# The scan's products of states and queries: one plain fp32 matmul each, or three passes over split operands

## The reference, cut to what matters

```python
states = jnp.einsum('bclgn,bclgr,bclgrp->bcgrpn', b_c, to_end, x_c)
chunk_decay = jnp.exp(a_cum[:, :, -1]).astype(dtype)
def carry_state(state, inp):
    st, dec = inp
    return state * dec[..., None, None] + st, state
_, h_in = lax.scan(carry_state, h0, (...states..., ...chunk_decay...))
y_off = jnp.einsum('bclgn,bcgrpn,bclgr->bclgrp', c_c, h_in, jnp.exp(a_cum).astype(dtype))
return (y_diag + y_off).reshape(bsz, s, g, r, p)
```

## Time and profile before

| | |
|---|---|
| time, median of 3 runs | 2360.77 us (2360.46 to 2361.38) |
| profiled execution | 2362.43 us |
| its span in the trace | 2360.6 us |
| mean granted TensorE clock over the span | 0.997 |
| instructions | 35337 |

### The profile page before, as it was taken

The page is one execution under the profiler, slowest core; times in us unless marked ns, Lnnn a source line. Parts: engine busy times, 40 slices in busy tenths (PEclk is TensorE's granted clock), DMA queues, the critical chain, the costliest instruction groups (busy, mean ns, idle before and its releaser), DMA issues.

```text
span 2360.6 us, 35337 instructions
## 1 busy us (share of the span) xinstructions
PE 2328.3 (99%) x14096; PEld 2017.1 (85%) x14096; DVE 1640.0 (69%) x2369; ACT 1241.5 (53%) x2034; POOL 267.1 (11%) x210
## 2 busy tenths in 40 slices
PE   8999999999999999999999999999999999999998
PEld 7777778766788888899988899998887888899997
DVE  5698846478775455687786788785677555777784
ACT  7777764355663344455554555554544354455552
POOL 0000000555100000100002200001033201100002
PEclk9999999999999999999999999999999999999999
DMA  6221335323566232233233243223322232333322
GB/s 199 81 72 52 89 106 176 118 74 113 188 217 213 86 125 67 90 113 108 90 99 107 81 125 108 87 84 108 115 64 63 90 116 72 107 108 108 93 69 90
DMA packets 177269, 251.97 MB, mean 107 GB/s; under 512 B 9936, under 2 KB 101328, under 8 KB 177104
## 3 DMA queue, kind: packets, MB, share of 16 engines
q1 hardware_dynamic: 175952, 248.13, 33.6%
q10 hardware_dynamic: 1152, 1.57, 0.2%
HBM read 231.83 MB, written 16.78 MB: 105 GB/s over the span
## 4 chain that ended last, share of the span: by engine, by line
PE 94%; DVE 3%; ACT 2%; issue 1%; DMA 1%; POOL 0%; SPq 0%; DVEq 0%; POOLq 0%; ACTq 0%
PE bank L1485 92%; PE bank L1647 1%; DVE wlo L2498 1%; PE bank L1670 0%; ACT whi L1886 0%; DMA zb<-scr_z 0%; PE bank L1768 0%; PE bank L1792 0%; DVE T L2506 0%; PE bank L1611 0%; DMA raw<-in_w_in 0%; DVE xg L2502 0%; ACT E L2153 0%; POOL xw L3411 0%; ACT pr L1887 0%
## 5 line engine op out<-in xcount | busy, mean ns | idle before, releaser
L1485 PE MATMUL bank<-xopr,shi 128*128 128x256 f32 x3360 | 605.0, 283 | 0.0
L1485 PEld LDWEIGHTS bank<-xopr,shi 128*128 128x128 f32 x3360 | 524.5, 192 | 0.5
L1485 PE MATMUL bank<-xopr,slo 128*128 128x256 f32 x1680 | 475.4, 283 | 0.0
L2498 DVE TENSOR_TENSOR wlo<-raw,whi 128x1024 fp32r<-128x1024 f32 (+2 forms) x286 | 351.7, 1234 | 128.3 <-ACT whi L1886 127.6
L1485 PE MATMUL bank<-xh,whi 128*128 128x512 f32 x1016 | 407.8, 401 | 7.2 <-DVE wlo L2498 7.2
L1485 PE MATMUL bank<-xh,wlo 128*128 128x512 f32 x1016 | 397.3, 391 | 0.0
L1485 PE MATMUL bank<-xl,whi 128*128 128x512 f32 x1016 | 397.2, 391 | 0.0
L1886 ACT ACTIVATE whi<-raw 128x1024 fp32r<-128x1024 f32 (+2 forms) x286 | 292.9, 1031 | 142.6 <-PE bank L1485 125.4
L1485 PEld LDWEIGHTS bank<-xopr,slo 128*128 128x128 f32 x1680 | 322.5, 192 | 0.0
L1485 PEld LDWEIGHTS bank<-xh,whi 128*128 128x128 f32 x1016 | 191.4, 188 | 49.8 <-DVE wlo L2498 8.1
L1485 PEld LDWEIGHTS bank<-xh,wlo 128*128 128x128 f32 x1016 | 191.1, 188 | 41.6
(11 more groups left out here) (396 smaller groups left out, 4341.9 us busy)
## 6 DMA issues: line engine op xcount, KB each, us to landing
raw<-in_w_in SPq DMA_DIRECT2D x92, 512.0 KB, 3.7
quarter<-in_w_ffn_in SPq DMA_DIRECT2D x32, 512.0 KB, 4.7
quarter<-in_ffn_gate SPq DMA_DIRECT2D x32, 512.0 KB, 3.8
quarter<-in_ffn_up SPq DMA_DIRECT2D x32, 512.0 KB, 4.8
raw<-in_ffn_down SPq DMA_DIRECT2D x28, 512.0 KB, 4.5
raw<-in_w_xattn_kv SPq DMA_DIRECT2D x16, 512.0 KB, 4.1
raw<-in_w_kv_mem SPq DMA_DIRECT2D x16, 512.0 KB, 4.7
raw<-in_w_branch_ssd SPq DMA_DIRECT2D x16, 512.0 KB, 4.7
```

The source lines that it names most:

```text
L1485: return e.matmul(out, l, r, start=start, stop=stop, skip_group_check=skip)
L2498: return e.tensor_tensor(out, a, b, op)
```

## The change

Each product of a state and the queries is made from split operands in three passes. ACT copies the queries of a group to `CTh` and each state to one of two buffers `Hh` as fp32r; DVE subtracts, and writes the lower parts in place: `CTl` over `CT`, `Hl` over `HF` or `HB`. `ct_split` is a step at the fourth state of a group, `h_split` number 0 at the sixth, and number k + 1 just ahead of product k.

```diff
+        Hl = [[None] + [at_kb(142 + 2 * i, [P, S], F32R, name="Hl") for i in range(3)],
+              [at_kb(148 + 2 * i, [P, S], F32R, name="Hl") for i in range(3)] + [None]]
+        Hh = [at_kb(kb, [P, S], F32R, name="Hh") for kb in (126, 214)]
+        CTh, CTl = at_kb(216, [P, S], F32R, name="CTh"), at_kb(190, [P, 4, S], F32R, name="CTl")
...
                 step("state", g, i)
+                if i == 3:
+                    step("ct_split", g)
+                if i == 5:
+                    step("h_split", g, 0)
                 yield
+        ACROSS = [(c, d) for c in range(4) for d in range(2) if (d, c) not in ((0, 0), (1, 3))]
...
+                    if (c, d) in ACROSS:
+                        k = ACROSS.index((c, d))
+                        if k < 5:
+                            step("h_split", g, k + 1)
                         side.new("off", g, c, d, among=ELSE)
                         step("across", g, c, d)
                         yield
...   (PE)
-                w.wait_ge(*at("h in", g, d, c))
-                mm(b[:], CT[:, g, chunk(c)], (HF, HB)[d][c][:], True, True).then_inc(*up("off", ("off", g, c, d)))
+                w.wait_ge(*at("ct lo", g))
+                w.wait_ge(*at("h lo", g, c, d))
+                hi = Hh[ACROSS.index((c, d)) % 2]
+                mm(b[:], CTh[:, chunk(c)], hi[:], True, False)
+                mm(b[:], CTh[:, chunk(c)], Hl[d][c][:], False, False)
+                mm(b[:], CTl[:, g, chunk(c)], hi[:], False, True).then_inc(*up("off", ("off", g, c, d)))
...   (ACT)
+            def ct_split(g):
+                w.wait_ge(*at("cb", g))
+                if g:
+                    w.wait_ge(*at("off", g - 1, 3, 0))
+                copy(CTh[:], CT[:, g, :]).then_inc(*up("h_first", ("ct hi", g)))
+            def h_split(g, k):
+                c, d = ACROSS[k]
+                w.wait_ge(*at("h in", g, d, c))
+                if k > 1:
+                    w.wait_ge(*at("off", g, *ACROSS[k - 2]))
+                elif g:
+                    w.wait_ge(*at("off", g - 1, 3, 0))
+                copy(Hh[k % 2][:], (HF, HB)[d][c][:]).then_inc(*up("h_first", ("h hi", g, c, d)))
...   (DVE)
+            def ct_split(g):
+                w.wait_ge(*at("ct hi", g))
+                tt(CTl[:, g, :], CT[:, g, :], CTh[:].bitcast(F32), ALU.subtract).then_inc(*up("h_in", ("ct lo", g)))
+            def h_split(g, k):
+                c, d = ACROSS[k]
+                w.wait_ge(*at("h decay", g, 5))
+                w.wait_ge(*at("h hi", g, c, d))
+                tt(Hl[d][c][:], (HF, HB)[d][c][:], Hh[k % 2][:].bitcast(F32), ALU.subtract).then_inc(
+                    *up("h_in", ("h lo", g, c, d)))
```

More of the change, by code:

```diff
@@ L834, in across @@
                 for d in range(2):
-                    if (d, c) not in ((0, 0), (1, 3)):
+                    if (c, d) in ACROSS:
+                        k = ACROSS.index((c, d))
+                        if k < 5:
+                            step("h_split", g, k + 1)
                         side.new("off", g, c, d, among=ELSE)
@@ L2477, in scalar @@
                     "k_split": k_split, "q_split": q_split,
-                    "o_split": o_split, "dt": dt, "cum": cum, "difference": difference, "pick": pick, "cb": cb, "state": state_, "decay": decay, "z_out": z_out,
+                    "o_split": o_split, "dt": dt, "cum": cum, "difference": difference, "pick": pick, "ct_split": ct_split, "h_split": h_split, "cb": cb, "state": state_, "decay": decay, "z_out": z_out,
                     "z_square": z_square, "y_mean": y_mean, "y_turn": y_turn, "bs_out": bs_out, "m_split": m_split,
@@ L3388, in vector @@
                     "conv_in": conv_in, "conv": conv, "silu_mul": silu_mul, "dt_turn": dt_turn, "gate": gate,
-                    "gate_out": gate_out, "o_split": o_split, "ba_out": ba_out, "dt": dt, "cum": cum, "difference": difference, "skip": skip,
+                    "gate_out": gate_out, "o_split": o_split, "ba_out": ba_out, "dt": dt, "cum": cum, "difference": difference, "ct_split": ct_split, "h_split": h_split, "skip": skip,
                     "state": state_, "decay": decay, "decayed": decayed, "y_add": y_add, "across": across_, "z_silu": z_silu, "z_gate": z_gate,
```

## The result

| | before | changed |
|---|---|---|
| median (range), 4 runs each | 2361.07 us (2360.46 to 2362.54) | 2382.95 us (2380.52 to 2383.63) |
| span of the profiled execution | 2360.6 us | 2381.8 us |
| granted clock over the span | 0.997 | 0.994 |

The ratio is 1.0091, 95% interval 1.0079 to 1.0103: the change costs 21.9 us. The forecast was slower by 8.0, with a range up to 2379. The sign held and the size didn't.

The account below looks back on a forecast made before the run. TensorE, busy 99%, bounds the kernel, with VectorE's chain beside or ahead of it late in the scan. Unabsorbed VectorE work 10.7, less lead 2.5, less group 0's 0.15, gives +8.0 us: 2368.8 us, range 2357 to 2379.

Parts of the forecast that it names:

- The bound by stage: Scan: chain VectorE, ScalarE, VectorE lies beside TensorE in groups 1 and 2, ahead in group 3; group 0 forecast at -0.15 us.
- the gain of 4.3 us: TensorE, 24 products: three passes take 0.69 us against 0.87 plain, 0.18 us less each, 1.1 us a group.
- The standing: VectorE in order at each split, waiting for ScalarE's upper part: 5.1 us a group, lower bound 2.4.
- The duration: VectorE's seven subtractions a group at 0.93 us each, 6.5 us a group; bounds 0.68 and 1.11 us each.
- The first product late by 0.8 us: Each group's first product waits longer for its state, by copy, subtraction and three semaphores: about 0.8 us, 0.95 in group 0.
- what can take it up: VectorE's waits for TensorE or POOL absorb its added work: 10.8, 7.6, 5.7 us in groups 1 to 3, leaving 10.7 together.
- The addition of 11.6 us a group: VectorE's added time in each of groups 1 to 3: 6.5 us of subtractions plus 5.1 us standing for ScalarE.
- the lead of 2.5 us: TensorE runs one point ahead of VectorE; using that up once without loss takes about 2.5 us off the sum.
- rival C: Scan: added waits cost more than their length through lower clock, no lead and 1.11 us subtractions; +17.7 us, 2378.5; chance 0.10.
- A: Rival: TensorE stays the bound, keeps its gain, and splits go into VectorE's waits in full; put at 2357.5 us; chance 0.22.
- B: Rival: gain and added work nearly cancel, by the lower bounds of VectorE's addition; +0.8 us, 2361.5; chance 0.17.
- D: Rival: three passes on TensorE with unhidden weight loads, +7.9 us instead of -4.3, 2369 by itself; chance 0.03.

## Why the prediction was wrong

**Held.** The bound by stage: TensorE pays where it waits for VectorE, group 0 nearly free (0.8 us), group 3 the dearest. The three passes at 0.23 us and the gain of 4.3 us (4.1 between the two runs without subtractions). The standing: 5.1 us a group forecast, 4.3, 4.6 and 5.9 us in the trace. In group 1 all of it is at the points with half 0 and at number 0; the 0.3 us at the others and at `ct_split` didn't appear. The duration: 0.93 us forecast; in groups 1 and 2 the backward states' subtractions took 1.25 and 1.10 us in the mean and the forward ones' 0.69, near the middle of the bounds. The seven of a group take 6.9, 6.4 and 5.1 us, so VectorE's addition is 11.2, 11.0 and 11.0 us, where 11.6 was forecast. The first product late by 0.8 us: TensorE waited 0.88, 0.64, 0.32 and 0.84 us for the four.

On the contention with POOL the trace agrees with the place in the Trainium skill cited in the prediction (SBUF — State Buffer, the paragraphs on the shared GPSIMD/Vector port). The subtraction that began at 490.95 beside a POOL operation recorded from 490.44 to 491.93 took 1.53 us, that is to the end of POOL's and 0.55 more; the one at 487.81, with POOL idle until 489.18, took 0.69.

**Failed: the step "what can take it up".** The addition of 11.6 us a group was nearly right. I let it vanish in all of VectorE's waits of the stretch, 10.8, 7.6 and 5.7 us, those for the states' products too. In the same stretches after, 5.7, 5.0 and 5.0 us of these waits still stand (beside the lines shown, `xg` 1.0 and the predicated copies 0.6 in group 2, `xg` 0.4 and, right behind 632, `T` 0.8 in group 3). So 8.4 us were taken up and not 24.1. With this number the forecast's own sum is 34.8 - 8.4 - 2.5 - 0.15 = 23.8 us, near the measured 21.9. The prediction had named this as a sign of being wrong: VectorE's waits for TensorE stay although the subtractions came.

The reason is the place. The work sits at the products, and there the wait is that of `yt`: 4.0, 4.2 and 1.8 us. A wait among the states, ahead of the added work, can't be spent on what isn't in the queue yet, and the one of the next group only as far as a lag is carried there; the waits that stayed say that little was carried. The rows had both numbers side by side. With those of `yt` alone:

| | group 1 | group 2 | group 3 |
|---|---|---|---|
| 11.6 less the wait of `yt` | 7.6 | 7.4 | 9.8 |
| less the lead of 2.5 us, once | 5.1 | 7.4 | 9.8 |
| measured | 5.0 | 7.8 | 9.0 |

The three groups make 22.3 us by this table and measured 21.8. The table was made after the result, and its third column is in part luck. Of the 1.8 us of `yt` in group 3, 1.3 are at the last product, behind the marker at 603.11, and weren't taken up (2.1 after). In their place VectorE's wait for ScalarE at `small`, a row that the prediction didn't count, went from 1.8 to 0.4 us, and the one for POOL from 2.7 to 1.7.

That the place matters was also tried: half of the subtractions moved among the states brought 4.9 us, a gain forecast as 3 to 6 us before the run, and there the waits for the states' products shrank by 2.8 us.

That the sums come out so closely owes something to terms that offset. TensorE's waits grew by about 16 us and its low clock by more than the forecast had (rival C's mechanism, which I gave 0.10 and 3.4 us): between 505 and 640 the windows' clocks make 12 us of lost full speed against 3.5 before, of which part lies inside the waits. How much of the 21.9 is clock alone stays open; no run takes the clock away and leaves the waits.

**Rivals.** A and B, in which the splits hide, are out for the changed kernel. D is out by the starts of the passes. C came nearest, at +17.7 us, and had the clock right in kind; but it got there by dropping the lead and by subtractions of 1.11 us, and kept the step that failed.

## What to carry to other kernels

Idle time of an engine is only room for work that is queued in it: take the waits between the points at which the added instructions stand, by the instruction that waits, and not the idle time of the stretch (here 8.4 us were taken up where 24.1 were counted on). An instruction that one engine makes from another's result puts two queues in series at that point; put the producer a step ahead in its own list, which here was worth 9 us without less work. Before splitting operands of small products, compare what TensorE gains with what the other engines pay: here 0.18 us a product against 1.3 us, 0.62 on ScalarE and 0.69 on VectorE.

## What wasn't expected of the hardware

A wait named after a bank wasn't ended by letting the products alternate over two, the second being shared (+26.0 against +21.9 us, 13.1 and 14.4 us of waiting for `yt`). The same subtraction of 128 by 512 took 0.69 us on VectorE and about 1.3 us on POOL. And waits of 1.34 and 4.00 us in TensorE, ended at 605.47 and 611.34, went with a granted clock of 0.68 and 0.50 over the ten microseconds from 605, where a single one of 1.51 us, ended at 527.47 in the kernel before, left it at 1.00. The length of one wait doesn't settle it: the one of 1.54 us before 589.66 went with 0.66.
